# A float32 hybrid decoder layer on Trainium2: x and the norms' vectors loaded by channel instead of transposed on chip

## The chip, the cores and the metric

The kernel runs on one core of one Trainium2 chip. The metric is the device time of the kernel in microseconds (us), as the median of several executions. Engines are named as in the profile: PE is TensorE's matmuls and PEld its weight loads, DVE is VectorE, ACT is ScalarE, POOL is GpSimd, and SP is the engine whose queue issues nearly all DMAs.

## What is computed

One decoder layer on x of 256 tokens by 2048 channels, float32, batch 1:

```python
h = x
h = _layer_norm(ALPHA * h + 0.5 * _swiglu(h, ffn1_w_gate, ffn1_w_up, ffn1_w_down), ln_ffn1_g, ln_ffn1_b)
h = _layer_norm(ALPHA * h + _mixer(h, w_in, ...), ln_mix_g, ln_mix_b)
h = _layer_norm(ALPHA * h + 0.5 * _swiglu(h, ffn2_w_gate, ffn2_w_up, ffn2_w_down), ln_ffn2_g, ln_ffn2_b)

def _swiglu(x, w_gate, w_up, w_down):
    return (silu(x @ w_gate) * (x @ w_up)) @ w_down      # 2048 -> 5632 -> 2048
```

The mixer (sparse attention, dilated attention and gates) isn't touched by the change, except that two of its position tables (cmp_k_pos, cmp_v_pos) are among the vectors whose loading changes.

## The kernel before

**Arithmetic.** Every product of float32 matrices is made of three: operands are split into a rounded part (hi, float32r) and the rest (lo), and hi*hi, lo*hi and hi*lo are summed in PSUM. Weights stream from memory in slots of 512 KB: 2 blocks of 128 rows by 512 columns. For each slot SP loads `raw`, ACT rounds it into `w_hi` (round_slot, L491), DVE subtracts to get `w_lo` (split_slot, L505), and PE makes 12 matmuls of 512 columns (multiply_slot, L511: eight with w_hi on L519 and L520, four with w_lo on L525). `raw`, `w_hi` and `w_lo` are rings of 4 slots.

**What orders the ring.** Counting semaphores do. The load of slot n waits until `lo_done` has reached n - 3, that is until the low part of slot n - 4 is made (load_slot, L469). The rounding of slot n waits until `slots_used` has reached n - 3, that is until PE has finished slot n - 4 (L501). DVE waits for `hi_done`, PE for `hi_done` and then `lo_done`. Each engine works strictly in the order in which its program is written.

**The first feed-forward layer.** gu_chunk runs over 11 chunks of 512 hidden columns. A chunk has 16 slots: 8 of the gate weights into one accumulator pair, 8 of the up weights into the other. Chunk 0 is written apart (peel). After the gate half's last slot PE increments `slots_used` to 8; ACT then takes the tanh of the accumulator (L841, at s = 9, in ACT's order behind the rounding of slot 9 and ahead of that of slot 10), and DVE multiplies (L1070, behind the low part of slot 9 and ahead of that of slot 10). Later chunks run in a loop, then four down chunks of 22 slots each read hT_hi and hT_lo.

**x in the first chunk.** The products need x by channel (128 channels on partitions, 256 tokens in the free dimension), split into act_hi and act_lo. x lies in memory by token. SP loads it by token into `resid` in five parts (load_x, L705, 1 KB or 2 KB pieces), which is also the residual that the down projection is added to. PE transposes a pair of channel blocks at a time, four transpositions into one PSUM bank (x_task, L1584; transpose_pair, L554 to L560), ACT rounds the bank into act_hi (x_pairs, L860, through round_pair, L598), DVE subtracts into act_lo (L1092, through split_pair, L608). Pair 0 is transposed ahead of slot 0, pair 1 behind slot 0's high products, and pair s + 1 in the middle of slot s for s = 1 to 6. The identity for it, 64 KB, is the second load of SP (L717). In front of and behind the first transposition PE makes 6 and 5 warm-up products on zeros (keep_warm, L1610). The first two weight slots are loaded in halves (first_weights, L710).

**The vectors.** Four norm vectors and two position tables are loaded by row behind the load of slot 4 (load_vectors, L734), transposed by PE behind the first chunk (setup_task, L1704) and copied to `vecT` by DVE at s = 11 (L1059). Their readers are the later norms on ACT and the block sums on POOL.

**SP's order.** The loads of chunk 0 with those of x in between; load_ln(0), two DMAs of 1 MB; the loop of chunks; the down weights; then the mixer's.

Of the kernel before, what the change touches and what calls it, by code (L numbers as in the profile page):

```python
# [46 lines left out]
WARM_START = (6, 5)  # L47
X_FIRST = 2
IN_HALVES = 2
X_PARTS = ((0, 256), (256, 512), (512, 1024), (1024, 1536), (1536, D))  # L50
# [76 lines left out]
class Plan:  # L127


    def __init__(self):  # L130
        self.k, self.uses, self.t, self.at, self.by_pos = 0, [0] * BANKS, {}, {}, {}
        self.turn = list(range(BANKS))
# [9 lines left out]
def plan():  # L142
# [115 lines left out]
def build(nc, x, w1_gate, w1_up, w1_down, ln1_g, ln1_b, w_in, ck_pos, ck_w1, ck_w2, cv_pos, cv_w1, cv_w2,  # L258
          w_a, w_b, w_o, ln2_g, ln2_b, w2_gate, w2_up, w2_down, ln3_g, ln3_b, rope_c, masks_c, small_c, out):

    (w1_gate, w1_up, w1_down, ln1_g, ln1_b, w_in, ck_pos, ck_w1, ck_w2, cv_pos, cv_w1, cv_w2, w_a, w_b, w_o,
     ln2_g, ln2_b, w2_gate, w2_up, w2_down, ln3_g, ln3_b) = (
        a[0] for a in (w1_gate, w1_up, w1_down, ln1_g, ln1_b, w_in, ck_pos, ck_w1, ck_w2, cv_pos, cv_w1, cv_w2,
# [4 lines left out]
    with ctx:  # L268
# [9 lines left out]
        pos_rows = sb("pos_rows", [CMP_BLOCK, 2, P])  # L278
# [5 lines left out]
        at = 1152 + 4 * (160 + 128 + 256 + 128 + 48 + 16 + 8)  # L284
# [105 lines left out]
        x_loaded = [sem(f"x_loaded{q}") for q in range(len(X_PARTS))]  # L390
# [313 lines left out]
        def _(sp):  # L704
            def load_x(q):  # L705
                cs = slice(*X_PARTS[q])
                sp.dma_start(resid[:, :, cs], x[0].rearrange("(t p) d -> p t d", p=P)[:, :, cs]) \
                    .then_inc(x_loaded[q], 16)
# [25 lines left out]
            def load_vectors():  # L734
                for v, a in enumerate((ln1_g, ln1_b, ln2_g, ln2_b)):
                    sp.dma_start(vec_rows[16 * v:16 * v + 16, :], a.rearrange("(t p) -> t p", p=P)) \
                        .then_inc(consts_loaded, 16)
                sp.dma_start(pos_rows[:, 0, :], ck_pos).then_inc(consts_loaded, 16)
                sp.dma_start(pos_rows[:, 1, :], cv_pos).then_inc(consts_loaded, 16)
# [82 lines left out]
        def _(act):  # L822
            def gu_chunk(f, i, peel):
                per, c0 = 2 * GU_SLOTS, gu_acc[f]
                for s in range(2 * GU_SLOTS):
                    if peel and f == 0 and s <= X_FIRST:
                        x_pairs(s)
# [4 lines left out]
                    if peel and f == 0 and X_FIRST < s < GU_SLOTS:  # L832
                        x_pairs(s)
# [26 lines left out]
            def x_pairs(j):  # L860

                round_pair(act, ("x", 0, j), pair_of(act_hi, 2 * j))
# [171 lines left out]
        def _(dve):  # L1034
# [8 lines left out]
            def gu_chunk(f, i, peel):  # L1043
                per = 2 * GU_SLOTS
                for s in range(2 * GU_SLOTS):
                    if peel and f == 0 and s <= X_FIRST:
                        x_pairs(s)
# [4 lines left out]
                    if peel and f == 0 and X_FIRST < s < GU_SLOTS:  # L1052
                        x_pairs(s)
                    if peel and f == 1 and SPLIT <= s < GU_SLOTS:
                        split_piece(1, s + SPLIT)
                    if f == 0 and peel and s == 11:
                        t = T[("setup",)]
                        wait_filled(dve, t)
                        nc.vector.tensor_copy(vecT[:, :], bank[:, t.bank, 0:128]).then_inc(bank_emptied[t.bank], 1)  # L1059
# [151 lines left out]
            def down(f):  # L1211

                n_slots = OUT_CHUNKS * DOWN_SLOTS
                for s in range(n_slots):
# [368 lines left out]
        def _(pe):  # L1583
            def x_task(f, j):  # L1584
                t = T[("x", f, j)]
                if f == 0:
                    if j == 0:
                        pe.wait_ge(small_loaded, 16)
                    if j < 2 or j % 2 == 0:
                        pe.wait_ge(x_loaded[j if j < 2 else j // 2 + 1], 16)  # L1590
                wait_bank_free(pe, t)
                transpose_pair(resid, 2 * P * j, t.bank)

# [16 lines left out]
            def keep_warm(n):  # L1610

                for _ in range(n):
                    nc.tensor.matmul(bank[:, 3, 0:P], hid[:, 0, 0:P], hid[:, 0, 0:P], start=True, stop=True)

            def first_chunk(n0, c0):

                pe.wait_ge(zeros_ready, 1)
                keep_warm(WARM_START[0])
                x_task(0, 0)
                keep_warm(WARM_START[1])  # L1620
                for s in range(GU_SLOTS):
                    wait_moved(pe, T[("x", 0, s)])
                    first_chunk_slot(s, c0 % 2)

            def first_chunk_slot(s, pair):
# [3 lines left out]
                if s < IN_HALVES:  # L1629
                    pe.wait_ge(half_rounded, s + 1)  # L1630
                else:
                    pe.wait_ge(hi_done, s + 1)
                for k in range(SLOT_KT):
                    if k and 0 < s < GU_SLOTS - 1:
                        x_task(0, s + 1)
                    if k and s < IN_HALVES:
                        pe.wait_ge(hi_done, s + 1)
                    hi = b_hi[:, k * COLS:(k + 1) * COLS]
# [64 lines left out]

            def setup_task():  # L1704

                t = T[("setup",)]
                pe.wait_ge(consts_loaded, 16 * 6)
                wait_bank_free(pe, t)
                nc.tensor.transpose(bank[:, t.bank, 0:64], vec_rows[:, :], ident[0:64, 0:64])
                nc.tensor.transpose(bank[:, t.bank, 64:96], pos_rows[:, 0, :], ident[0:32, 0:32])  # L1710
                nc.tensor.transpose(bank[:, t.bank, 96:128], pos_rows[:, 1, :], ident[0:32, 0:32]).then_inc(bank_filled, 1)
# [300 lines left out]
        def _(pool):  # L2012
# [6 lines left out]

            for v in range(2):  # L2020
# [15 lines left out]
_INS = ["x", "ffn1_w_gate", "ffn1_w_up", "ffn1_w_down", "ln_ffn1_g", "ln_ffn1_b", "w_in", "cmp_k_pos", "cmp_k_w1",  # L2036
        "cmp_k_w2", "cmp_v_pos", "cmp_v_w1", "cmp_v_w2", "w_branch_a", "w_branch_b", "w_o", "ln_mix_g", "ln_mix_b",
        "ffn2_w_gate", "ffn2_w_up", "ffn2_w_down", "ln_ffn2_g", "ln_ffn2_b"]

# [16 lines left out]
```

## Time and profile before

| | |
|---|---|
| Median of 3 executions | 2217.81 us (2217.52 to 2217.85) |
| The profiled execution, its own time | 2217.98 us |
| Its span, first to last instruction | 2216.2 us |
| Mean granted clock of TensorE | 0.998 |
| Busy: PE, DVE, ACT | 2201.7 us, 1235.7 us, 959.6 us |
| Moved by DMA | 422.86 MB, mean 191 GB/s |

The rows below come from this one profiled execution. Starts are counted from the first instruction. A row of the timeline has the start, the duration, the engine, the line of the kernel, the operation, output and inputs, the shape and the count of what was merged; in brackets stands how long the engine had been idle and what released it. A matmul's duration contains its way through the array, so matmuls overlap: the distance between starts is what one costs. The granted clock (PEclk) is 1.00 for 2.4 GHz and 0.50 for 1.2 GHz.

### The profile page before, as it was taken

What the parts mean: (1) busy time and instruction counts of PE and PEld (TensorE: products, weight loads), DVE (VectorE), ACT (ScalarE), POOL (GpSimd) and SP (SyncE); (2) the same over time, 40 slices, a digit from 0 to 9 for tenths busy, and PEclk for the clock granted to TensorE, in tenths of its full rate; (3) what the DMA queues carried; (4) which work ended last, traced back from release to release, by engine and by line L of the source; (5) the groups of instructions that cost most, each with busy time, mean ns of one, the idle gap of its engine ahead of it and who ended that gap; (6) DMA issues with size and microseconds to landing.
All of it is one profiled execution on the core that took longest, in us unless ns stands there. A gap on an engine that the chain in (4) does not pass through costs nothing.

```text
span 2216.2 us, 27207 instructions
## 1 busy us (share of the span) xinstructions
PE 2201.7 (99%) x10137; PEld 1823.6 (82%) x10137; DVE 1235.7 (56%) x1230; ACT 959.6 (43%) x1126; POOL 7.7 (0%) x12
## 2 busy tenths in 40 slices
PE   9999999999999999999999999999999999999998
PEld 7888888888888888888888888888888888888886
DVE  5555455544544776776654556567555545545445
ACT  4344434443333644544345444364444444443333
POOL 0000000000000010000000000000000000000000
PEclk9999999999999999999999999999999999999999
DMA  7655665565666666665557566656655566566664
GB/s 270 206 184 188 190 191 185 188 191 190 195 192 193 186 188 206 188 184 161 169 163 208 171 204 206 196 166 195 197 188 180 188 197 188 180 236 193 196 191 142
DMA packets 224860, 422.86 MB, mean 191 GB/s; under 512 B 16400, under 2 KB 25872, under 8 KB 224016
## 3 DMA queue, kind: packets, MB, share of 16 engines
q1 hardware_dynamic: 224208, 420.76, 61.7%
q8 instruction: 52, 0.85, 0.2%
q10 hardware_dynamic: 576, 1.05, 0.1%
q14 instruction: 24, 0.20, 0.0%
HBM read 418.08 MB, written 3.68 MB: 190 GB/s over the span
## 4 chain that ended last, share of the span: by engine, by line
PE 98%; DVE 1%; ACT 0%; DMA 0%; issue 0%; SPq 0%; DVEq 0%; ACTq 0%
PE acc L519 31%; PE acc L520 31%; PE acc L525 31%; PE bank L558 1%; PE bank L1903 1%; PE bank L1743 0%; PE bank L1852 0%; PE bank L1874 0%; PE acc L1640 0%; PE acc L1641 0%; PE bank L1957 0%; PE acc L1647 0%; PE bank L1954 0%; DMA raw<-in_ffn_w_gate_dram 0%; PE bank L1856 0%; DVE w_lo L509 0%
## 5 line engine op out<-in xcount | busy, mean ns | idle before, releaser
L509 DVE TENSOR_TENSOR w_lo<-raw,w_hi 128x1024 fp32r<-128x1024 f32 x768 | 928.3, 1224 | 572.3 <-ACT w_hi L502 564.5
L502 ACT ACTIVATE w_hi<-raw 128x1024 fp32r<-128x1024 f32 x766 | 802.9, 1059 | 820.9 <-PE acc L525 775.0
L519 PE MATMUL acc<-w_hi,act_hi 128*128 128x512 f32 x2192 | 865.9, 395 | 0.0
L520 PE MATMUL acc<-w_hi,act_lo 128*128 128x512 f32 x2192 | 854.3, 390 | 0.0
L525 PE MATMUL acc<-w_lo,act_hi 128*128 128x512 f32 x2192 | 588.2, 389 | 0.1
L525 PEld LDWEIGHTS acc<-w_lo,act_hi 128*128 128x128 f32 x2192 | 411.3, 188 | 87.4 <-DVE w_lo L509 1.0
L519 PEld LDWEIGHTS acc<-w_hi,act_hi 128*128 128x128 f32 x2192 | 411.7, 188 | 86.7 <-issue 3.2
L520 PEld LDWEIGHTS acc<-w_hi,act_lo 128*128 128x128 f32 x2192 | 411.9, 188 | 82.1
L519 PE MATMUL acc<-w_hi,hT_hi 128*128 128x512 f32 x688 | 267.9, 389 | 0.0
L520 PE MATMUL acc<-w_hi,hT_lo 128*128 128x512 f32 x688 | 267.7, 389 | 0.0
L525 PE MATMUL acc<-w_lo,hT_hi 128*128 128x512 f32 x688 | 185.2, 389 | 0.0
L525 PEld LDWEIGHTS acc<-w_lo,hT_hi 128*128 128x128 f32 x688 | 129.2, 188 | 26.8
L520 PEld LDWEIGHTS acc<-w_hi,hT_lo 128*128 128x128 f32 x688 | 129.2, 188 | 26.7
L519 PEld LDWEIGHTS acc<-w_hi,hT_hi 128*128 128x128 f32 x688 | 129.1, 188 | 26.7
L1089 DVE TENSOR_TENSOR hT_lo<-bank,hT_hi 128x512 f32 (+1 forms) x44 | 30.3, 688 | 97.2 <-ACT hT_hi L858 97.2
L1070 DVE SCALAR_TENSOR_TENSOR gate_t<-gate_t,acc 128x1024 f32<-128x1024 f32 x22 | 26.9, 1222 | 88.7 <-ACT gate_t L841 88.7
L858 ACT ACTIVATE hT_hi<-bank 128x512 f32 (+1 forms) x44 | 26.2, 595 | 108.0 <-PE bank L558 108.0
L1081 DVE TENSOR_TENSOR hid<-gate_t,acc 128x1024 f32<-128x1024 f32 x22 | 26.9, 1222 | 65.0 <-PE acc L525 65.0
L841 ACT ACTIVATE gate_t<-acc 128x1024 f32<-128x1024 f32 x22 | 22.6, 1029 | 92.1 <-PE acc L525 90.1
L519 PE MATMUL acc<-w_hi,oT_hi 128*128 128x512 f32 x96 | 38.0, 395 | 0.0
L520 PE MATMUL acc<-w_hi,oT_lo 128*128 128x512 f32 x96 | 37.4, 390 | 0.0
L689 ACT ACTIVATE s<-s,negmax 128x128 f32<-128x128 f32 (+1 forms) x56 | 23.8, 430 | 26.8 <-DVE negmax L1310 26.8
(243 smaller groups left out, 842.2 us busy)
## 6 DMA issues: line engine op xcount, KB each, us to landing
raw<-in_ffn_w_up_dram SPq DMA_DIRECT2D x176, 512.0 KB, 4.5
raw<-in_ffn_w_down_dram SPq DMA_DIRECT2D x176, 512.0 KB, 4.5
raw<-in_w_in_dram SPq DMA_DIRECT2D x176, 512.0 KB, 4.2
raw<-in_ffn_w_gate_dram SPq DMA_DIRECT2D x174, 512.0 KB, 4.5
raw<-in_w_o_dram SPq DMA_DIRECT2D x32, 512.0 KB, 4.8
raw<-in_w_branch_a_dram SPq DMA_DIRECT2D x16, 512.0 KB, 5.1
raw<-in_cmp_k_w_dram SPq DMA_DIRECT2D x8, 512.0 KB, 4.0
raw<-in_cmp_v_w_dram SPq DMA_DIRECT2D x8, 512.0 KB, 4.0
```

The source lines that it names most:

```text
L502: nc.scalar.activation(weights(n0, s if isinstance(i, int) and i == 0 else s + per)[0], raw[:, r, :], ACT.Copy).then_inc(hi_done, 1)
L509: nc.vector.tensor_tensor(lo, raw[:, r, :], hi.bitcast(F32), ALU.subtract).then_inc(lo_done, 1)
L519: nc.tensor.matmul(o, a_hi[:, kt0 + k, at], hi, start=first and k == 0, stop=False)
L520: nc.tensor.matmul(o, a_lo[:, kt0 + k, at], hi, start=False, stop=False)
L525: mm = nc.tensor.matmul(o, a_hi[:, kt0 + k, at], lo, start=False, stop=last and k == SLOT_KT - 1)
L558: mm = nc.tensor.transpose(bank[:, b, k * TOKENS + tile * P:k * TOKENS + (tile + 1) * P], src[:, tile, col + k * P:col + (k + 1) * P], ident)
L689: nc.scalar.activation(v, v, ACT.Exp, bias=negmax[:, u, e:e + 1], scale=SCALE, accum_out=sums[:, u, e:e + 1]).then_inc(probs_ready, 1)
L841: nc.scalar.activation(gate_t[:, :, :], acc_pair(0), ACT.Tanh, scale=0.5).then_inc(gate_tanh, 1)
L858: nc.scalar.activation(dst, bank[:, half, :].rearrange("p (k n) -> p k n", k=2), ACT.Copy).then_inc(hi_moved, 1)
L1070: nc.vector.scalar_tensor_tensor(gate_t[:, :, :], gate_t[:, :, :], 1.0, acc_pair(0), ALU.add, ALU.mult).then_inc(acc_emptied[0], 1)
L1081: nc.vector.tensor_tensor(hid[:, :, :], gate_t[:, :, :], acc_pair(1), ALU.mult).then_inc(acc_emptied[1], 1)
L1089: nc.vector.tensor_tensor(hT_lo[:, k0, :], bank[:, half, :].rearrange("p (k n) -> p k n", k=2), hT_hi[:, k0, :].bitcast(F32), ALU.subtract ...
```

## The change

x is handed to the kernel in two layouts. Besides x by token there is a copy by channel (xT_c: row p holds, for each of the 16 channel blocks, the 256 tokens of channel p of the block), and one array vec_c that already holds what `vecT` has to hold. The kernel loads eight pairs of x by channel into x_raw, in memory that the hidden activations use later, each just ahead of the weights of its slot. ACT rounds and DVE subtracts from x_raw instead of from PSUM. The transpositions of x and of the vectors on PE are gone, and so is the copy of `vecT` on DVE. Eight warm-up products come in one group. x by token is loaded into `resid` in one DMA of 2 MB by SP behind the loop of chunks, ahead of the down weights, and DVE waits for it before the first add. The identity and `vecT` are loaded by load_constants, which SP reaches behind gu_chunk(0, 0) and ahead of load_ln(0); PE waits for the identity behind the first chunk, where the setup transposition was; ACT and POOL wait for `vecT` before they read it.

Since no bank is used for x any longer, the counts of tasks and of bank uses start at 1 instead, fed by the last warm-up product and by two memsets.

```diff
-WARM_START = (6, 5)
+WARM_START = 8
...
-        self.k, self.uses, self.t, self.at, self.by_pos = 0, [0] * BANKS, {}, {}, {}
+        self.k, self.uses, self.t, self.at, self.by_pos = 1, [1, 1, 0, 0], {}, {}, {}
...
-        for j in range(GU_SLOTS):
+        for j in range(GU_SLOTS if f else 0):
             task(("x", f, j), j % BANKS)
-        if f == 0:
-            task(("setup",), 2)
...
+        x_raw = chunks_lo[:, 0:4].rearrange("p a t (k n) -> p (a t k) n", n=TOKENS)
...
@@ sync
+            def load_x(j):
+                sp.dma_start(pair_of(x_raw, 2 * j), xT_c[:, 2 * j * TOKENS:(2 * j + 2) * TOKENS]).then_inc(x_loaded[j], 16)
...
-            load_x(0)
-            sp.dma_start(ident, small_c[:, n_small:]).then_inc(small_loaded, 16)
...
                         peel = f == 0 and isinstance(i, int) and h == 0
+                        if peel:
+                            load_x(s)
                         if peel and s < IN_HALVES:
                             first_weights(s)
                         else:
                             load_slot(sp, src, gu_slot[f], i, 2 * GU_SLOTS, h * GU_SLOTS + s)
-                        if peel:
-                            for q in ((1,), (2,), (), (3, 4))[s] if s < 4 else ():
-                                load_x(q)
-                            if s == 4:
-                                load_vectors()
...
+            def load_constants():
+                sp.dma_start(ident, small_c[:, n_small:]).then_inc(small_loaded, 16)
+                sp.dma_start(vecT[:, :], vec_c).then_inc(consts_loaded, 16)
 
             def ffn(f):
                 gu_chunk(f, 0)
                 if f == 0:
+                    load_constants()
                     load_ln(0)
                 with sp.Fori(1, GU_CHUNKS) as i:
                     gu_chunk(f, i)
-                if f == 1:
+                if f == 0:
+                    sp.dma_start(resid[:, :, :], x[0].rearrange("(t p) d -> p t d", p=P)).then_inc(resid_loaded, 16)
+                else:
                     sp.wait_ge(resid_ready, 2)
                     load_ln(2)
...
@@ scalar: x_pairs(s) stands ahead of the rounding of slot s for all s < 8
-                round_pair(act, ("x", 0, j), pair_of(act_hi, 2 * j))
+                act.wait_ge(x_loaded[j], 16)
+                nc.scalar.activation(pair_of(act_hi, 2 * j), pair_of(x_raw, 2 * j), ACT.Copy).then_inc(hi_moved, 1)
...
             def layer_norm_act(which):
+                act.wait_ge(consts_loaded, 16)
...
@@ vector: the same order
-                split_pair(dve, ("x", 0, j), pair_of(act_lo, 2 * j), pair_of(act_hi, 2 * j))
+                dve.wait_ge(hi_moved, moved[("x", 0, j)] + 1)
+                nc.vector.tensor_tensor(pair_of(act_lo, 2 * j), pair_of(x_raw, 2 * j), pair_of(act_hi, 2 * j).bitcast(F32),
+                                        ALU.subtract).then_inc(x_split, 1)
...
+                        if c == 0 and f == 0:
+                            dve.wait_ge(resid_loaded, 16)
...
+            for b in range(2):
+                nc.vector.memset(ln_s[:, 0, b:b + 1], 0.0).then_inc(bank_emptied[b], 1)
...
@@ tensor
-                keep_warm(WARM_START[0])
-                x_task(0, 0)
-                keep_warm(WARM_START[1])
+                keep_warm(WARM_START)
                 for s in range(GU_SLOTS):
-                    wait_moved(pe, T[("x", 0, s)])
                     first_chunk_slot(s, c0 % 2)
...
                 for k in range(SLOT_KT):
-                    if k and 0 < s < GU_SLOTS - 1:
-                        x_task(0, s + 1)
...
+                    pe.wait_ge(hi_moved, moved[("x", 0, s)] + 1)
                     for o, at in outs:
                         nc.tensor.matmul(o, act_hi[:, 2 * s + k, at], hi, start=s == 0 and k == 0, stop=False)
+                    pe.wait_ge(x_split, s + 1)
+                    for o, at in outs:
                         nc.tensor.matmul(o, act_lo[:, 2 * s + k, at], hi, start=False, stop=False)
-                if s == 0:
-                    x_task(0, 1)
...
                             first_chunk(n0, c0)
-                            setup_task()
+                            pe.wait_ge(small_loaded, 16)
...
@@ gpsimd
+            pool.wait_ge(consts_loaded, 16)
```

## Rows read from the trace of the kernel before

**Rows 1.** The page's first part: busy time of each engine.
```profile
PE 2201.7 (99%) x10137; PEld 1823.6 (82%) x10137; DVE 1235.7 (56%) x1230; ACT 959.6 (43%) x1126; POOL 7.7 (0%) x12
```
**Rows 2.** Waits of PE, whole execution: us in total, times, longest.
```profile
PE bank L1957 <- DVE w_lo L509: 1.1, 2, 0.8
...
PE acc L1640 <- ACT w_hi L848: 0.5, 1, 0.5
...
PE acc L1640 <- ACT w_hi L850: 0.4, 1, 0.4
```
**Rows 3.** Timeline of PE, start to 40 us: start, duration, what.
```profile
1.06 2.93 PE L1613 MATMUL bank<-hid 128*128 128x128 f32 x12 [1.06 <-DVE ln_s L1257]
...
4.46 1.28 PE L1613 MATMUL bank<-hid 128*128 128x128 f32 x10
...
10.87 0.50 PE L1640 MATMUL acc<-w_hi,act_hi 128*128 128x512 f32 x1 [0.49 <-DVE act_lo L608]
...
30.32 0.39 PE L1640 MATMUL acc<-w_hi,act_hi 128*128 128x512 f32 x1
...
32.13 1.07 PE L1647 MATMUL acc<-w_lo,act_hi 128*128 128x512 f32 x4
...
33.57 0.50 PE L519 MATMUL acc<-w_hi,act_hi 128*128 128x512 f32 x1
...
35.52 1.07 PE L525 MATMUL acc<-w_lo,act_hi 128*128 128x512 f32 x4
...
38.24 1.07 PE L525 MATMUL acc<-w_lo,act_hi 128*128 128x512 f32 x4
```
**Rows 4.** DMA issues at 1.26 and 2.23: count, size, us to landing.
```profile
small<-in_small_dram SPq DMA_DIRECT2D x1, 64.0 KB, 2.6
...
raw<-in_ffn_w_gate_dram SPq DMA_DIRECT2D x1, 256.0 KB, 4.9
```
**Rows 5.** Timeline of ACT in the first chunk and behind it.
```profile
7.14 0.63 ACT L850 ACTIVATE w_hi<-raw 128x512 fp32r<-128x512 f32 x1 [1.06 <-DMA raw<-in_ffn_w_gate_dram]
9.49 0.60 ACT L598 ACTIVATE act_hi<-bank 128x512 fp32r<-128x512 f32 x1 [1.71 <-PE bank L558]
...
33.24 1.03 ACT L841 ACTIVATE gate_t<-acc 128x1024 f32<-128x1024 f32 x1 [2.07 <-PE acc L1647]
34.16 2.00 ACT L502 ACTIVATE w_hi<-raw 128x1024 fp32r<-128x1024 f32 x2
```
**Rows 6.** Timeline of DVE in the first chunk and behind it.
```profile
7.88 1.23 DVE L509 TENSOR_TENSOR w_lo<-raw,w_hi 128x1024 fp32r<-128x1024 f32 x1 [1.91 <-ACT w_hi L850]
10.12 0.69 DVE L608 SCALAR_TENSOR_TENSOR act_lo<-bank,act_hi 128x512 fp32r<-128x512 f32 x1 [1.02 <-ACT act_hi L598]
...
34.30 1.22 DVE L1070 SCALAR_TENSOR_TENSOR gate_t<-gate_t,acc 128x1024 f32<-128x1024 f32 x1 [1.69 <-ACT gate_t L841]
35.44 2.35 DVE L509 TENSOR_TENSOR w_lo<-raw,w_hi 128x1024 fp32r<-128x1024 f32 x2
```
**Rows 7.** Windows: PE, PEld, DVE, ACT, POOL busy (count), PEclk, DMA share, GB/s.
```profile
13.00:14.00 1.00, 1.00 (x6) 0.75 (x4) 0.69 (x1) 1.00 (x3) 0.00 (x0) 1.00 1.07 416
```
**Rows 8.** Timeline of SP: loads of the up half, and the next DMA.
```profile
19.49 18.70 SPq L474 DMA_DIRECT2D raw<-in_ffn_w_up_dram  x8
38.23 0.47 SPq L759 DMA_DIRECT2D ln_nat<-in_ln_ffn_g_dram  x1
```
**Rows 9.** DMA landings: slot 15 (issued at 37.8), ln_nat behind it, median of all up loads.
```profile
raw<-in_ffn_w_up_dram SPq DMA_DIRECT2D x1, 512.0 KB, 6.8
ln_nat<-in_ln_ffn_g_dram SPq DMA_DIRECT2D x1, 1024.0 KB, 8.3
...
raw<-in_ffn_w_up_dram SPq DMA_DIRECT2D x176, 512.0 KB, 4.5
```
**Rows 10.** The last matmuls, and the window in which the granted clock falls.
```profile
2205.01 0.61 PE L525 MATMUL acc<-act_lo,hT_hi 128*128 128x512 f32 x2
...
2209.00:2209.50 0.50, 0.00 (x0) 0.00 (x0) 0.50 (x1) 0.44 (x2) 0.00 (x0) 0.55 0.00 0
```

More of the change, by code:

```diff
@@ L45 @@
 LAST_SPLIT = 8
-WARM_START = (6, 5)
-X_FIRST = 2
+WARM_START = 8
 IN_HALVES = 2
-X_PARTS = ((0, 256), (256, 512), (512, 1024), (1024, 1536), (1536, D))
 SPLIT = 4
@@ L255, in mixer_constants, with build @@
             np.ascontiguousarray(small, np.float32))
-def build(nc, x, w1_gate, w1_up, w1_down, ln1_g, ln1_b, w_in, ck_pos, ck_w1, ck_w2, cv_pos, cv_w1, cv_w2,
+def build(nc, x, xT_c, vec_c, w1_gate, w1_up, w1_down, ln1_g, ln1_b, w_in, ck_w1, ck_w2, cv_w1, cv_w2,
           w_a, w_b, w_o, ln2_g, ln2_b, w2_gate, w2_up, w2_down, ln3_g, ln3_b, rope_c, masks_c, small_c, out):
-    (w1_gate, w1_up, w1_down, ln1_g, ln1_b, w_in, ck_pos, ck_w1, ck_w2, cv_pos, cv_w1, cv_w2, w_a, w_b, w_o,
+    (w1_gate, w1_up, w1_down, ln1_g, ln1_b, w_in, ck_w1, ck_w2, cv_w1, cv_w2, w_a, w_b, w_o,
      ln2_g, ln2_b, w2_gate, w2_up, w2_down, ln3_g, ln3_b) = (
-        a[0] for a in (w1_gate, w1_up, w1_down, ln1_g, ln1_b, w_in, ck_pos, ck_w1, ck_w2, cv_pos, cv_w1, cv_w2,
+        a[0] for a in (w1_gate, w1_up, w1_down, ln1_g, ln1_b, w_in, ck_w1, ck_w2, cv_w1, cv_w2,
                        w_a, w_b, w_o, ln2_g, ln2_b, w2_gate, w2_up, w2_down, ln3_g, ln3_b))
@@ L277, in build @@
         vec_rows = sb("vec_rows", [64, P])
-        pos_rows = sb("pos_rows", [CMP_BLOCK, 2, P])
         vecT = sb("vecT", [P, 4 * KT + 2 * CMP_BLOCK])
@@ L282, in build @@
         mv = sb("mv", [P, TILES, 2])
-        at = 1152 + 4 * (160 + 128 + 256 + 128 + 48 + 16 + 8)
+        at = 1152 + 4 * (160 + 128 + 128 + 48 + 16 + 8)
         if at % 512:
@@ L389, in build @@
         hi_moved = sem("hi_moved")
-        x_loaded = [sem(f"x_loaded{q}") for q in range(len(X_PARTS))]
+        x_loaded = [sem(f"x_loaded{j}") for j in range(GU_SLOTS)]
+        x_split = sem("x_split")
+        resid_loaded = sem("resid_loaded")
         small_loaded = sem("small_loaded")
@@ L704, in _ @@
         def _(sp):
[L705 to L708, printed above, removed]
+            def load_x(j):
+                sp.dma_start(pair_of(x_raw, 2 * j), xT_c[:, 2 * j * TOKENS:(2 * j + 2) * TOKENS]).then_inc(x_loaded[j], 16)
             def first_weights(s):
@@ L727, in gu_chunk @@
                             load_slot(sp, src, gu_slot[f], i, 2 * GU_SLOTS, h * GU_SLOTS + s)
-                        if peel:
-                            for q in ((1,), (2,), (), (3, 4))[s] if s < 4 else ():
-                                load_x(q)
-                            if s == 4:
-                                load_vectors()
[L734 to L739, printed above, removed]
+            def load_constants():
+                sp.dma_start(ident, small_c[:, n_small:]).then_inc(small_loaded, 16)
+                sp.dma_start(vecT[:, :], vec_c).then_inc(consts_loaded, 16)
             def ffn(f):
@@ L825, in gu_chunk @@
                 for s in range(2 * GU_SLOTS):
-                    if peel and f == 0 and s <= X_FIRST:
+                    if peel and f == 0 and s < GU_SLOTS:
                         x_pairs(s)
@@ L831, in gu_chunk @@
                         round_slot(act, gu_slot[f], i, per, s)
-                    if peel and f == 0 and X_FIRST < s < GU_SLOTS:
-                        x_pairs(s)
                     if peel and f == 1 and SPLIT <= s < GU_SLOTS:
@@ L1045, in gu_chunk @@
                 for s in range(2 * GU_SLOTS):
-                    if peel and f == 0 and s <= X_FIRST:
+                    if peel and f == 0 and s < GU_SLOTS:
                         x_pairs(s)
@@ L1051, in gu_chunk @@
                         split_slot(dve, gu_slot[f], i, per, s)
-                    if peel and f == 0 and X_FIRST < s < GU_SLOTS:
-                        x_pairs(s)
                     if peel and f == 1 and SPLIT <= s < GU_SLOTS:
                         split_piece(1, s + SPLIT)
[L1056 to L1059, printed above, removed]
                     if peel and f == 1 and s >= 10:
@@ L1583, in _ @@
         def _(pe):
[L1584 to L1592, printed above, removed]
             def norm_task(f, j):
@@ L1612, in keep_warm @@
                 for _ in range(n):
-                    nc.tensor.matmul(bank[:, 3, 0:P], hid[:, 0, 0:P], hid[:, 0, 0:P], start=True, stop=True)
+                    mm = nc.tensor.matmul(bank[:, 3, 0:P], hid[:, 0, 0:P], hid[:, 0, 0:P], start=True, stop=True)
+                mm.then_inc(bank_filled, 1)
             def first_chunk(n0, c0):
                 pe.wait_ge(zeros_ready, 1)
-                keep_warm(WARM_START[0])
-                x_task(0, 0)
-                keep_warm(WARM_START[1])
+                keep_warm(WARM_START)
                 for s in range(GU_SLOTS):
-                    wait_moved(pe, T[("x", 0, s)])
                     first_chunk_slot(s, c0 % 2)
@@ L1628, in first_chunk_slot @@
                 outs = [(acc[:, 2 * pair + tile, :], slice(tile * P, (tile + 1) * P)) for tile in range(TILES)]
[L1629 to L1632, printed above, removed]
                 for k in range(SLOT_KT):
-                    if k and 0 < s < GU_SLOTS - 1:
-                        x_task(0, s + 1)
-                    if k and s < IN_HALVES:
+                    hi = b_hi[:, k * COLS:(k + 1) * COLS]
+                    if s < IN_HALVES and k == 0:
+                        pe.wait_ge(half_rounded, s + 1)
+                    else:
                         pe.wait_ge(hi_done, s + 1)
-                    hi = b_hi[:, k * COLS:(k + 1) * COLS]
+                    pe.wait_ge(hi_moved, moved[("x", 0, s)] + 1)
                     for o, at in outs:
                         nc.tensor.matmul(o, act_hi[:, 2 * s + k, at], hi, start=s == 0 and k == 0, stop=False)
+                    pe.wait_ge(x_split, s + 1)
+                    for o, at in outs:
                         nc.tensor.matmul(o, act_lo[:, 2 * s + k, at], hi, start=False, stop=False)
-                if s == 0:
-                    x_task(0, 1)
                 pe.wait_ge(lo_done, s + 1)
@@ L1702, in gu_chunk @@
                                 h_task(f, i, half)
[L1704 to L1711, printed above, removed]
             def ffn(f):
@@ L2033, in _, with by_partition @@
                 ins.then_inc(blk_ready, 1)
-_INS = ["x", "ffn1_w_gate", "ffn1_w_up", "ffn1_w_down", "ln_ffn1_g", "ln_ffn1_b", "w_in", "cmp_k_pos", "cmp_k_w1",
-        "cmp_k_w2", "cmp_v_pos", "cmp_v_w1", "cmp_v_w2", "w_branch_a", "w_branch_b", "w_o", "ln_mix_g", "ln_mix_b",
+_INS = ["ffn1_w_gate", "ffn1_w_up", "ffn1_w_down", "ln_ffn1_g", "ln_ffn1_b", "w_in", "cmp_k_w1", "cmp_k_w2",
+        "cmp_v_w1", "cmp_v_w2", "w_branch_a", "w_branch_b", "w_o", "ln_mix_g", "ln_mix_b",
         "ffn2_w_gate", "ffn2_w_up", "ffn2_w_down", "ln_ffn2_g", "ln_ffn2_b"]
+def by_partition(a):
+    n = a.shape[0]
+    return np.ascontiguousarray(a.reshape(n, -1, P).transpose(2, 1, 0)).reshape(P, -1)
 def kernel(**inputs):
@@ L2045 @@
     nc = bacc.Bacc("TRN2", target_bir_lowering=False, num_devices=1, dynamic_dma_scratch_size=1024)
-    named = [(name, np.ascontiguousarray(inputs[name])) for name in _INS]
+    x = np.ascontiguousarray(inputs["x"])
+    vectors = [by_partition(np.asarray(inputs[name])) for name in ("ln_ffn1_g", "ln_ffn1_b", "ln_mix_g", "ln_mix_b")]
+    vectors += [np.asarray(inputs[name])[0].T for name in ("cmp_k_pos", "cmp_v_pos")]
+    named = [("x", x), ("x_by_channel", by_partition(x[0])), ("vectors", np.ascontiguousarray(np.concatenate(vectors, 1)))]
+    named += [(name, np.ascontiguousarray(inputs[name])) for name in _INS]
     named += list(zip(("rope", "masks", "small"), mixer_constants()))
```

## The prediction, on record before the changed kernel was run

> **What bounds the kernel now.** I read the page's busy times first: TensorE is busy for 99% of the span, VectorE for little more than half [rows 1]. The waits of TensorE come next: the largest group behind the very first instruction is 1.1 us in two pieces, and the others are waits of about half a microsecond for the first slots' operands [rows 2]. So TensorE's own work is the time, and a change pays only by taking work off TensorE or by removing the few gaps at the front, and it costs whatever new wait it gives TensorE. The third view is the order of TensorE's instructions at the start [rows 3]. Two groups of low-part products lie 2.72 us apart where nothing but weights is multiplied (35.52 and 38.24): that is a slot of twelve matmuls, 0.227 us each, and every slot of the first chunk above this is what the change can win. The slots of the first chunk take longer: from 10.87 to 30.32 there are six of them, 3.24 us each.
>
> **Step 1, slot 0.** Before, slot 1 begins at 10.87 [rows 3]. Ahead of it stand the second half of slot 0's weights (issued at 2.23, 4.9 us to landing, so 7.13 [rows 4]), its rounding from 7.14 for 0.63 [rows 5], its low part on VectorE from 7.88 for 1.23 [rows 6], then transposition, rounding and splitting of x's second pair in series. Afterwards the identity's load no longer stands ahead of the weights: two SP issues of about 0.5 us become one, and 64 KB go. The second half is issued at about 1.72. With the same 4.9 us it lands at 6.6; x now comes in 2 KB pieces per partition instead of 1 KB ones and there is less in front, so I take 6.3. Rounding to 6.98, low part from 7.1 to 8.3, its four matmuls to 9.3. The second pair of x is there as raw channels, so its rounding (0.60 us [rows 5]) and its split (0.69 [rows 6]) run under slot 0, and slot 1 begins at 9.3. Bounds: 9.0 and 10.4 (the old time less the 0.5 us of the issue, if x or slot 1's halves are what comes last). The eight warm-up calls are 16 passes from 1.06 on; they end before the first product, as the old ones did, and cost nothing; the weights cover them.
>
> **Step 2, slots 1 to 7.** The six transpositions between the products go: 19.45 us for six slots becomes 6 x 2.72 = 16.32, a gain of 3.1. From slot 7's start to its last group it is 1.81 (30.32 to 32.13), unchanged. So the last group of the first chunk, call its start M, moves from 32.13 to 9.3 + 16.32 + 1.81 = 27.43: 4.7 us earlier. What could eat this are the transfers: 768 KB are wanted per 2.72 us, 290 GB/s, against 416 GB/s where the queues are full [rows 7]. ACT spends 0.60 + 1.0 us and DVE 0.69 + 1.2 on a slot with its x pair [rows 5, 6]. Both fit; I charge 0.
>
> **Step 3, the setup transposition.** Before, the up half begins at 33.57, M + 1.44; the four matmuls of M's group need 0.91. So removing the three small transpositions gives 0.53.
>
> **Step 4, the new wait, the largest term.** Behind the first chunk TensorE waits for small_loaded, and the identity is now loaded by load_constants, which SP reaches only after it has issued all 16 slots of chunk 0. SP does not run that far ahead. The load of slot 15 waits for the low part of slot 11; slot 11 is rounded only when slot 7 is used up, and ACT does the gate's tanh first. The trace shows this chain: tanh at 33.24, two roundings from 34.16 [rows 5]; the gate's product on DVE at 34.30, two low parts from 35.44 for 2.35 [rows 6], thus to 37.79; then the eighth up load, and at 38.23 the next DMA in SP's order, ln_nat [rows 8]. That is the place the identity takes: M + 6.10. None of this chain waits for the up half of TensorE, so it is no deadlock, and nothing in it gets shorter. With M at 27.43 the issue is at 33.53. Queued behind the waiting TensorE are all products of the up half; ACT and DVE follow to slot 11 and then stand too, having no used slot to refill. Hence nothing is recouped.
> The landing of the identity at that place is not in the trace. At the kernel's start the same 64 KB took 2.6 us [rows 4]. Slot 15's 512 KB, issued 0.4 us before our place, took 6.8 us, with ln_nat's 2 MB behind it [rows 9]; the identity has those 2 MB behind it too. These are the bounds; I take 4.2, a little nearer the low one, since a small transfer need not wait for all of the large one's stragglers. TensorE resumes at 33.53 + 4.2 = 37.73 where it was at 33.57: +4.2 with steps 1 to 3 included (-5.2 for them, +9.4 for the wait).
> The Trainium skill (DMA: Bandwidth & Descriptors, Queues, rings and completion order) says that a DMA's semaphore lands only after every earlier write of the same engine. By that the identity cannot be seen before slot 15 is in, and the sum would be that of the third rival; no row here shows a small load right behind such a large one.
>
> **Step 5, the clock.** TensorE stands for some 9 us. At the end of the kernel its last matmuls start at 2205.01, and the granted clock falls from 1.00 to 0.50, the 1.2 GHz level, within 2209.0 to 2209.5 [rows 10], less than 4 us after them. So it restarts at half speed. How long this lasts shows at the kernel's start: 12 passes took 2.93 us, 0.24 each, the later 10 took 1.28, 0.13 each [rows 3]; the column says 1.00 there, but the durations say half. Half of 2.93 is lost: +1.5. Bounds 0 (it may come back at once) and 3.0 (twice as long).
>
> **At nothing.** x by token, 2 MB on SP before the down weights: ln_nat's 2 MB behind chunk 0 delay the following slots in just this way and no wait of TensorE shows there [rows 2]; the first reader is some 60 us later. If the ring's lead were gone it would cost up to 5 us (2 MB at 416 GB/s). vecT by DMA takes one copy off DVE; its new waits on ACT and POOL come tens of us after it. Two more memsets on DVE at the start are under 0.1 us each, under the loads. The plan's banks and turns stay as they were, so the mixer is untouched.
>
> **Sum.** The profiled execution took 2217.98 (span 2216.2); 2217.98 + 4.2 + 1.5 = 2223.7. The median of the runs is 0.17 lower; I give 2223.6.
>
> **Rivals.** First, on the other side: SP has the identity issued in time, so TensorE goes from chunk to chunk without a stop. Place: SP's order behind slot 15. Price: no wait, no clock loss, -5.2, 2212.8. For it: steps 1 to 3 are read from rows, and SP does run about four slots ahead elsewhere. Against: slot 15's load hangs on slot 11's low part, and the issue at M + 6.1 is a row. It decides when wait and clock together are under 5.2 us, which needs an issue about 3 us or more before that place even with the shortest landing.
> Second, a short wait: landing in 2.6 us and a clock that is back within 1 us: 2217.98 + 2.6 + 0.5 = 2221.1, no difference to be measured. For it: the identity is small, and the start shows 2.6. Against: up to two 512 KB loads stand in front.
> Third, a long wait: the identity lands with slot 15, which before was at 37.8 + 6.8 = 44.6, or M + 12.5. TensorE resumes at 39.9: +6.3, with the clock 1.5: 2225.8. For it: the 6.8 itself. Against: the median landing of all 176 up loads is 4.5 us [rows 9], and the 2 MB of ln_nat now come about 1 us later.
>
> **How the numbers follow.** A measurement can tell about 0.2%, 4.4 us. The forecast, landing within about 3 to 5 us, has 0.50; the long wait 0.28; the short one 0.18; no wait 0.04. So slower 0.78, within 0.2% 0.18, faster 0.04. With all low bounds the sum is +2.3 (front -0.3, landing -1.6, clock -1.5), with all high ones +10.9; both ends need everything at once. The range holds the middle of each: 2220.8 to 2227.4, leaving out the first rival and the extreme corners.
>
> **What would show it.** TensorE's waits list a new one of 8 to 11 us at the first matmul of the up half, released by the DMA into small; SP issues that DMA about 6.1 us behind the start of the last first-chunk group; a stretch of granted clock 0.50 begins in the gap, and the first products behind it have twice the distance. First-chunk slots are 2.72 us apart from about 9.3, with M near 27.4. The landing of the identity is the term to read first. The forecast is wrong if the identity is issued well before the first chunk ends, if a second wait shows in the first chunk (x or weights late), or if the down projection waits for its weights behind x by token.

## The result, and the profile after

| | before | after |
|---|---|---|
| Median | 2217.86 us (2217.52 to 2218.12, 8 runs) | 2225.23 us (2224.57 to 2226.54, 8 runs) |
| Profiled execution | 2217.98 us | 2226.54 us |
| Span, mean granted clock | 2216.2 us, 0.998 | 2224.7 us, 0.996 |

The ratio is 1.0033, with a 95% interval of 1.0024 to 1.0042: the change makes the kernel slower by 7.4 us. Forecast were 2223.6 us and slower; the time lies inside the range, 1.6 us above the forecast. The profiled execution of after is the slowest of its eight, so its terms below add up to 8.6 us, not 7.4.

The lines of the changed file have moved: what was L501 to L525 is one line less, L1640 and L1641 are L1617 and L1620, L1647 is L1624, L1613 is L1595, the tanh L841 is L831, the gate product L1070 is L1056.

TensorE's waits over the whole execution, as [rows 2] for before (us in total, times, longest):

```profile
PE acc L518 <- DMA small<-in_small_dram: 10.1, 1, 10.1
...
PE acc L1617 <- ACT w_hi L501: 0.8, 1, 0.8
PE acc L1617 <- ACT w_hi L838: 0.6, 1, 0.6
PE acc L524 <- DVE w_lo L508: 0.3, 1, 0.3
```

The first line is new and is by itself larger than the whole loss. Its place is in the timeline of TensorE, which answers to [rows 3]:

```profile
1.06 3.53 PE L1595 MATMUL bank<-hid 128*128 128x128 f32 x16 [1.06 <-DVE ln_s L1249]
5.21 0.73 PE L1617 MATMUL acc<-w_hi,act_hi 128*128 128x512 f32 x2 [0.62 <-ACT w_hi L838]
...
8.42 0.72 PE L1617 MATMUL acc<-w_hi,act_hi 128*128 128x512 f32 x2
...
12.35 0.73 PE L1617 MATMUL acc<-w_hi,act_hi 128*128 128x512 f32 x2 [0.81 <-ACT w_hi L501]
...
26.09 0.62 PE L1617 MATMUL acc<-w_hi,act_hi 128*128 128x512 f32 x2
...
27.90 1.07 PE L1624 MATMUL acc<-w_lo,act_hi 128*128 128x512 f32 x4
39.05 0.79 PE L518 MATMUL acc<-w_hi,act_hi 128*128 128x512 f32 x1 [10.08 <-DMA small<-in_small_dram]
39.64 0.63 PE L519 MATMUL acc<-w_hi,act_lo 128*128 128x512 f32 x1
40.07 0.63 PE L518 MATMUL acc<-w_hi,act_hi 128*128 128x512 f32 x1
...
46.56 1.07 PE L524 MATMUL acc<-w_lo,act_hi 128*128 128x512 f32 x4
47.47 0.39 PE L518 MATMUL acc<-w_hi,act_hi 128*128 128x512 f32 x1
```

The last group of the first chunk starts at 27.90 instead of 32.13: the front works. Then TensorE stands until 39.05, and its first products behind that are 0.43 us apart instead of 0.23.

The chain that holds the identity, in the timelines of ACT, DVE and SP, as [rows 5, 6, 8]:

```profile
29.01 1.02 ACT L831 ACTIVATE gate_t<-acc 128x1024 f32<-128x1024 f32 x1 [4.25 <-PE acc L1624]
29.93 1.99 ACT L501 ACTIVATE w_hi<-raw 128x1024 fp32r<-128x1024 f32 x2
44.63 1.06 ACT L501 ACTIVATE w_hi<-raw 128x1024 fp32r<-128x1024 f32 x1 [12.71 <-PE acc L524]
```

```profile
30.07 1.22 DVE L1056 SCALAR_TENSOR_TENSOR gate_t<-gate_t,acc 128x1024 f32<-128x1024 f32 x1 [4.05 <-ACT gate_t L831]
31.20 2.36 DVE L508 TENSOR_TENSOR w_lo<-raw,w_hi 128x1024 fp32r<-128x1024 f32 x2
45.72 1.23 DVE L508 TENSOR_TENSOR w_lo<-raw,w_hi 128x1024 fp32r<-128x1024 f32 x1 [12.17 <-ACT w_hi L501]
```

```profile
17.46 16.49 SPq L473 DMA_DIRECT2D raw<-in_ffn_w_up_dram  x8
33.99 0.47 SPq L727 DMA_DIRECT2D small<-in_small_dram  x1
```

Tanh, two roundings, gate product, two low parts, slot 15's load, identity: the same order as before, and the issue is 6.09 us behind the start of the last group, where ln_nat stood 6.10 behind it [rows 8]. ACT and DVE then stand for 12 us as well (12.71 and 12.17 in brackets), so no work is done ahead by which the stop could be made good later.

DMA landings of slot 15's load (issued at 33.59) and of the identity behind it, and windows of the granted clock (PEclk is the third number from the end):

```profile
raw<-in_ffn_w_up_dram SPq DMA_DIRECT2D x1, 512.0 KB, 5.2
small<-in_small_dram SPq DMA_DIRECT2D x1, 64.0 KB, 5.0
```

```profile
31.50:32.00 0.50, 0.00 (x0) 0.00 (x0) 0.50 (x1) 0.42 (x1) 0.00 (x0) 0.50 0.00 0
...
43.00:44.00 1.00, 1.00 (x4) 0.75 (x3) 0.00 (x0) 0.00 (x0) 0.00 (x0) 0.50 0.14 57
45.00:45.50 0.50, 0.50 (x3) 0.37 (x3) 0.00 (x0) 0.50 (x1) 0.00 (x0) 0.85 0.00 0
```

The clock is at 0.50 (1.2 GHz) from 31.5 on and comes back shortly after 45.0, six microseconds behind the restart.

### The profile page after: what moved, and what is told of

It is laid out like the page before. It is cut to its first block, busy times and chain, and to the rows that moved or that the text cites. A ratio compares the mean times of both kernels' runs of the same rounds, so it can differ in the third digit from the quotient of the medians.

```text
span 2224.7 us, 27140 instructions
## 1 busy us (share of the span) xinstructions
PE 2199.9 (99%) x10096; PEld 1821.2 (82%) x10096; DVE 1235.6 (56%) x1231; ACT 959.4 (43%) x1126; POOL 7.7 (0%) x12
## 4 chain that ended last, share of the span: by engine, by line
PE 97%; DVE 1%; DMA 1%; ACT 0%; SPq 0%; issue 0%; DVEq 0%; ACTq 0%
PE acc L518 31%; PE acc L519 30%; PE acc L524 30%; PE bank L557 1%; PE bank L1871 1%; PE bank L1711 0%; PE bank L1820 0%; PE bank L1842 0%; DVE w_lo L508 0%; DMA raw<-in_ffn_w_gate_dram 0%; PE bank L1925 0%; PE bank L1922 0%; PE acc L1617 0%; PE acc L1624 0%; PE acc L1620 0%; DMA small<-in_small_dram 0%
## 5 line engine op out<-in xcount | busy, mean ns | idle before, releaser
L501 ACT ACTIVATE w_hi<-raw 128x1024 fp32r<-128x1024 f32 x766 | 802.4, 1058 | 835.2 <-PE acc L524 776.9
L518 PE MATMUL acc<-w_hi,act_hi 128*128 128x512 f32 x2192 | 867.1, 396 | 10.1 <-DMA small<-in_small_dram 10.1
L1056 DVE SCALAR_TENSOR_TENSOR gate_t<-gate_t,acc 128x1024 f32<-128x1024 f32 x22 | 26.9, 1221 | 91.1 <-ACT gate_t L831 91.1
L831 ACT ACTIVATE gate_t<-acc 128x1024 f32<-128x1024 f32 x22 | 22.6, 1028 | 94.3 <-PE acc L524 90.1
```

Source lines behind the costliest of these rows:

```text
L501: nc.scalar.activation(weights(n0, s if isinstance(i, int) and i == 0 else s + per)[0], raw[:, r, :], ACT.Copy).then_inc(hi_done, 1)
L518: nc.tensor.matmul(o, a_hi[:, kt0 + k, at], hi, start=first and k == 0, stop=False)
L831: nc.scalar.activation(gate_t[:, :, :], acc_pair(0), ACT.Tanh, scale=0.5).then_inc(gate_tanh, 1)
L1056: nc.vector.scalar_tensor_tensor(gate_t[:, :, :], gate_t[:, :, :], 1.0, acc_pair(0), ALU.add, ALU.mult).then_inc(acc_emptied[0], 1)
```

## The experiments

The theory was that the late identity and the clock it costs are the whole loss, and that the front gains some 5 us. Rivals: that x by token or the new traffic costs something too; that the slow products behind the stop have another cause; that a DMA of 64 KB has its own latency of 5 us; that the transpositions were not what the front gained. The ratios stand against the kernel before on the same chip, 2217.95 us for the first four runs and 2217.85 us for the last four.

**The wait moved to its first use.**

```diff
-                            pe.wait_ge(small_loaded, 16)
...
                         if not peel and h == 0 and s == 3:
+                            if f == 0:
+                                pe.wait_ge(small_loaded, 16)
                             for half in range(2):
                                 h_task(f, i, half)
```

> The changed kernel with TensorE's wait for the identity moved from behind the first chunk to its first use, the transposition of the hidden activations in the loop. Loads stay where they are. My theory (the late identity and the clock drop are the whole loss): no stop behind the first chunk, granted clock 1.00 throughout the front, about 4.9 us faster than the kernel before (first chunk's last group at 27.9 where it was at 32.13, 4.2, and 0.5 for the setup transposition), 2213.0 us. Rival (x by token ahead of the down weights, or the bigger traffic, costs something of its own, hidden now by the stop's refilled ring): a new wait appears later and the gain is under 4 us, 2214 us or more.

Measured: 2213.32 us (2212.63 to 2213.89), ratio 0.9979 (0.9970 to 0.9988). Its timeline of TensorE across the end of the first chunk:

```profile
27.95 1.07 PE L1624 MATMUL acc<-w_lo,act_hi 128*128 128x512 f32 x4
28.86 0.39 PE L518 MATMUL acc<-w_hi,act_hi 128*128 128x512 f32 x1
```

One wait moved by some 30 us of TensorE's own work turns 7.4 us lost into 4.6 us won. The up half starts 4.71 us earlier than before (28.86 for 33.57), and the profiled execution, 2213.32 us, is 4.66 us below the profiled one of before. So nothing of the front's gain is given back later: x by token, 2 MB more, is hidden, as charged.

**The constants issued early.** SP runs load_constants() behind the load of slot 7, the wait stays behind the first chunk.

```diff
+                        if peel and s == GU_SLOTS - 1:
+                            load_constants()
...
                 if f == 0:
-                    load_constants()
                     load_ln(0)
```

> The changed kernel with the identity and vecT issued by SP behind the load of slot 7 instead of behind slot 15; TensorE's wait stays behind the first chunk. My theory: the identity is issued near 16 us and has landed long before 28.8 us even in full queues, so the same time as with the wait moved, 2213.0 us within 0.5. Rival (a wait there costs by itself, or the two loads delay the weights of the first chunk): 1 us or more above that run.

Measured: 2213.57 us (2212.58 to 2214.12), ratio 0.9979 (0.9970 to 0.9988), the same as with the wait moved. A wait for something that has landed costs nothing that shows here; place of issue and place of wait are two cures for one fault.

**TensorE kept busy in the gap.**

```diff
                             first_chunk(n0, c0)
+                            for _ in range(38):
+                                nc.tensor.matmul(bank[:, 3, 0:P], hid[:, 0, 0:P], hid[:, 0, 0:P], start=True, stop=True)
                             pe.wait_ge(small_loaded, 16)
```

> The changed kernel with 38 more warm-up products of zeros behind the first chunk, ahead of the wait for the identity. They take about 9.5 us of the 10.1 us in which TensorE stands, so the stop is as long but the clock should stay up. My theory: the granted clock stays 1.00, TensorE resumes at about 39.0 us as before but at full distance, and the time falls by what the clock cost: 3.0 us against the profiled execution of the changed kernel, 2 to 3 us against its median: 2222.2 to 2223.2 us. Rival (the slow first products behind the stop are due to something else, such as the DMA traffic then): no change, 2225 us.

Measured: 2223.46 us (2223.09 to 2225.81), ratio 1.0026 (1.0016 to 1.0035). TensorE:

```profile
28.90 8.64 PE L1670 MATMUL bank<-hid 128*128 128x128 f32 x76
38.49 0.50 PE L518 MATMUL acc<-w_hi,act_hi 128*128 128x512 f32 x1 [0.94 <-DMA small<-in_small_dram]
38.83 0.40 PE L519 MATMUL acc<-w_hi,act_lo 128*128 128x512 f32 x1
39.07 0.40 PE L518 MATMUL acc<-w_hi,act_hi 128*128 128x512 f32 x1
```

The window behind the stop, PEclk third from the end:

```profile
39.00:40.00 1.00, 1.00 (x6) 0.77 (x6) 0.00 (x0) 0.00 (x0) 0.00 (x0) 1.00 1.03 434
```

76 products whose result is not used make the kernel 1.8 us faster than the change by the medians, a little under the 2 to 3 us expected, and the products behind the stop are back at 0.23 us. The granted clock stayed at 1.00 while the DMAs moved as much as behind the stop of the changed kernel (434 and 395 GB/s from 39 to 40). So the clock was the cause of the slow products, and not the traffic. From resuming to the low-part group of the second up slot it takes 4.70 us here (38.49 to 43.19) and 7.51 in the changed kernel (39.05 to 46.56): 2.8 us in that execution. The medians say 1.8; the cost differs from run to run. The next kernel gives the cleanest pair: its TensorE resumes at the same 38.49 with the clock at 0.50, takes 6.83 us over the same two slots, 2.13 more, and its profiled execution is longer by 2.13 us as well (2225.22 and 2223.09).

**The identity without the 2 MB behind it.**

```diff
                 sp.dma_start(ident, small_c[:, n_small:]).then_inc(small_loaded, 16)
+                sp.wait_ge(small_loaded, 16)
                 sp.dma_start(vecT[:, :], vec_c).then_inc(consts_loaded, 16)
```

> The changed kernel with SP waiting for the identity before it issues vecT and ln_nat, so that no 2 MB are queued behind it. SP's place of issue stays, near 34.0 us. If the traffic behind the identity delayed it (slot 15 took 5.2 us, the identity 5.0): it lands in about 3.5 us and TensorE resumes 1.5 us earlier, about 2223.7 us. If what counts is what stands ahead of it (slots 14 and 15) or a fixed latency: 5.0 us to landing as before, 2225.2 us.

Measured: 2225.16 us (2224.4 to 2226.3), ratio 1.0032 (1.0020 to 1.0043), no change. The identity took 4.6 us instead of 5.0. What stands behind it hardly matters (3.5 us was expected if it did), so what is left is what stands ahead of it, or a latency of its own.

**The identity ahead of slot 15.**

```diff
+                        if f == 0 and isinstance(i, int) and h == 1 and s == GU_SLOTS - 2:
+                            sp.dma_start(ident, small_c[:, n_small:]).then_inc(small_loaded, 16)
...
             def load_constants():
-                sp.dma_start(ident, small_c[:, n_small:]).then_inc(small_loaded, 16)
```

> The changed kernel with the identity issued by SP between the loads of slots 14 and 15, one DVE low part (1.2 us) earlier than in the change. In the changed kernel it landed 0.2 us behind slot 15's 512 KB, which was issued just ahead of it. If a small load is seen only once the large load ahead of it is in: it now lands just behind slot 14, whose load took 3.6 us from 32.4, at about 36.2 us; TensorE resumes some 2.8 us earlier and the time is 2222.4 us. If the landing is a latency of its own of about 5 us: issue near 32.8, landing near 37.8, 1.2 us earlier, 2224.0 us.

Measured: 2222.74 us (2221.90 to 2223.52), ratio 1.0021 (1.0012 to 1.0030), 2.5 us below the change where 2.8 were expected. Landings of slot 14's load (issued at 33.17) and of the identity (33.58):

```profile
raw<-in_ffn_w_up_dram SPq DMA_DIRECT2D x1, 512.0 KB, 3.7
small<-in_small_dram SPq DMA_DIRECT2D x1, 64.0 KB, 3.5
```

The identity's time to landing fell from 5.0 to 3.5 us, with the load ahead of it: 33.58 + 3.5 = 37.1, slot 14 at 36.9. In the profiles of all four kernels with the stop it landed 0.1 to 0.3 us behind the large load in front. It has no latency of its own of 5 us; it was seen when the load ahead of it was in. The Trainium skill (DMA: Bandwidth & Descriptors, Queues, rings and completion order) says that the increment of a DMA's semaphore lands only after every earlier write of the same DMA engine, and that DMAs of one issuing engine need not complete in their order for all that. The four traces agree with the first; no run here shows the second.

**Slot 2's weights in halves too**, on the kernel with the wait at its use.

```diff
-IN_HALVES = 2
+IN_HALVES = 3
```

> The kernel with the wait at its use, and slot 2's weights loaded and rounded in halves like those of slots 0 and 1 (IN_HALVES 3). TensorE stood 0.9 us ahead of slot 2 for its rounding. If the half's earlier landing and its shorter rounding (0.63 instead of 1.06 us) are what was late: the wait falls to 0.3 us or less and the time by 0.5 us or more, 2212.8 us. If the transfer of the whole slot is the limit: the wait moves to the second half, no change, 2213.3 us.

Measured: 2212.42 us (2212.0 to 2213.74), ratio 0.9975 (0.9966 to 0.9985), 5.4 us below the kernel before and the fastest version found. It is 0.9 us below the kernel with the wait at its use, by medians of 10 and 11 runs whose ranges overlap (2212.0 to 2213.74 and 2212.63 to 2213.89). No wait ahead of slot 2 is left in its profile, but that execution, the slowest of the ten, ran the whole of slot 0 at half speed, which hides such a wait. So the 0.9 us rest on the medians, and that they are this wait is likely and not shown.

**The transpositions put back**, on the kernel with the wait at its use. The transposed data are zeros and aren't used.

```diff
+                    if k == 0 and 0 < s < GU_SLOTS - 1:
+                        pe.wait_ge(small_loaded, 16)
+                        for q in range(4):
+                            nc.tensor.transpose(bank[:, 3, q * P:(q + 1) * P], hid[:, 0, 0:P], ident)
...
+            act.dma_start(ident, small_c[:, TILES * N_CMP + TILES:]).then_inc(small_loaded, 16)
```

> The kernel with the wait at its use, with four transpositions of zeros into a free bank put back into the middle of each of slots 1 to 6, as the kernel before had them; the identity is loaded by ACT's queue at the start, and the results are not used. In the kernel before, such slots took 3.20 instead of 2.72 us. If this was the transpositions' own price: 6 x 0.48 = 2.9 us, less up to 0.5 us that slot 1's hide in the wait ahead of slot 2: 2215.9 to 2216.3 us. If the chain from transposition over ACT and DVE back to TensorE was part of it: less than 2.0 us, under 2215.3 us.

Measured: 2216.63 us (2215.05 to 2217.09), ratio 0.9993 (0.9984 to 1.0002). Slots 3 and 4 in its timeline:

```profile
16.69 0.62 PE L1617 MATMUL acc<-w_hi,act_hi 128*128 128x512 f32 x2
17.14 0.62 PE L1620 MATMUL acc<-w_hi,act_lo 128*128 128x512 f32 x2
17.60 0.60 PE L1624 MATMUL bank<-small,hid 128*128 128x128 f32 x4
17.96 0.71 PE L1617 MATMUL acc<-w_hi,act_hi 128*128 128x512 f32 x2
...
19.89 0.62 PE L1617 MATMUL acc<-w_hi,act_hi 128*128 128x512 f32 x2
```

That is 3.20 us per slot with no consumer of the result. Before the change slots 3 to 6 took the same, from here to slot 7's start at 30.32:

```profile
17.51 0.39 PE L1640 MATMUL acc<-w_hi,act_hi 128*128 128x512 f32 x1
```

So the price in these slots was TensorE's own time, 0.48 us for four transpositions and the change of operand, and not the chain over ACT and DVE. The median is 3.3 us above the kernel without them, 0.3 to 0.7 more than expected. In the profile the first product comes at 5.73 instead of 5.20 and slot 0 runs at half speed; the extra load of the identity at the start may be behind the first, and it wasn't tried alone.

**x's pairs 1 and 2 on ACT's queue**, on the same kernel.

```diff
                         if peel and s not in (1, 2):
                             load_x(s)
...
+            for j in (1, 2):
+                act.dma_start(pair_of(x_raw, 2 * j), xT_c[:, 2 * j * TOKENS:(2 * j + 2) * TOKENS]).then_inc(x_loaded[j], 16)
             act.wait_ge(zeros_ready, 3)
```

> The kernel with the wait at its use, with x's pairs 1 and 2 issued by ACT's queue at the start instead of by SP, so that SP issues slot 2's weights about 1 us earlier. If the issue rate limits the first slots: the 0.9 us ahead of slot 2 disappear, 2212.5 us. If the rate of the transfers does (about 300 GB/s from 4 to 9 us): the wait stays above 0.6 us, and slot 0 may even start later because x competes with its weights, 2213.3 us or more.

Measured: 2214.73 us (2214.29 to 2215.64), ratio 0.9985 (0.9976 to 0.9994), 1.4 us slower than the kernel with the wait at its use. TensorE's first product, and a window behind it:

```profile
6.68 0.73 PE L1619 MATMUL acc<-w_hi,act_hi 128*128 128x512 f32 x2 [2.07 <-ACT w_hi L838]
```

```profile
8.00:9.00 1.00, 1.00 (x3) 0.81 (x4) 1.00 (x1) 1.00 (x3) 0.00 (x0) 0.50 1.04 404
```

It starts at 6.68 instead of 5.20, because ACT began to round x's pair 0 at 4.93 instead of 3.88 and slot 0's weights at 6.00 instead of 4.52, both released by their loads. The loads that TensorE needs first land 1.1 to 1.5 us later when more is issued beside them. What was to disappear did: slot 2's weights are rounded at 9.76 instead of 11.30, and no wait of TensorE stands ahead of that slot. But the granted clock fell to 0.50 between 7.5 and 8 and came back at about 11, so that slot 0 took 4.58 us and not 3.40, and the up half starts at 30.34 instead of 28.86. The issue order, the queue and the clock all changed, so this run doesn't tell whether the issue or the transfers made slot 2 late. It does show that some 300 GB/s was no ceiling: from 2 to 9 us it moved 336 GB/s, where the kernel with the wait at its use moved 291.

## Why the prediction was right, and where it was off

The sum against the profiled execution, in us (the forecast's last step is rounded up: 2223.68 less 0.17 is 2223.5, and 2223.6 was given):

| Term | Forecast | Measured |
|---|---|---|
| First chunk (27.90 for 32.13) and setup transposition (0.53), steps 1 to 3 | -5.2 | -4.8 |
| Stop: issue behind the last group's start | 6.10 | 6.09 |
| Stop: from issue to TensorE's resumption | 4.2 | 5.06 |
| Stop in all (step 4) | +9.4 | +10.2 |
| Clock (step 5) | +1.5 | +2.8 |
| Sum | +5.7 | +8.2, of 8.6 in all |

The other 0.3 us were not found. The front, the landing and the clock all came out worse than forecast. That the median is only 1.6 us off is in part because the profiled execution is the slowest of its eight: by the medians the clock cost 1.8.

**Mechanism and sign.** The prediction named the stop, the order of SP that causes it, and its length to within 0.9 us. The place of issue was right to 0.01 us, and not by luck: it is 6.09 us in the kernels with TensorE busy in the gap and with the identity alone too. It came from finding what stood at that place in the trace of before, and from checking that nothing in the chain to it depends on the work that the wait holds up.

One of the prediction's own signs of being wrong did show: a second wait in the first chunk, 0.8 us ahead of slot 2, for weights that were late. It belongs to step 2 and is small beside the stop.

**Step 1** was too late by 0.9: slot 1 began at 8.42, not 9.3, because the second half of the weights was being rounded at 5.33 (6.3 was the landing taken, [rows 4] had 7.1).

**Step 2** was too hopeful where it charged 0 for transfers. From slot 1 to slot 2 it was 3.93 us, not 2.72: slot 2's weights took 7.2 us from their issue at 4.05, and ACT could round them only at 11.24. The 416 GB/s of [rows 7] is the rate at 13 us; from 4 to 8 us both kernels move 239 to 332 GB/s. The two errors go against each other and leave the last group at 27.90 for 27.43. Loading and rounding slot 2 in halves then won 0.9 by the medians.

**Step 4's landing** was mis-sized: 5.0 for 4.2. I had put it nearer the low bound because a small transfer need not wait for all of a large one's stragglers. Here it did: the identity landed with the load ahead of it in every such profile. The third rival had the mechanism right. Its number, 6.4 us, was too long only because slot 15 itself took 5.2 us this time and not 6.8; why, no run shows (4.6 and 4.9 in two of the other kernels with the stop).

The prediction says that no row shows a small load right behind a large one. The trace of before had such rows. At its start, the load of x ahead of the identity was issued at 0.75:

```profile
resid<-in_x_dram SPq DMA_DIRECT2D x1, 256.0 KB, 2.9
small<-in_small_dram SPq DMA_DIRECT2D x1, 64.0 KB, 2.6
```

It lands at 3.65 and the identity, issued at 1.26, at 3.86, 0.2 us behind it: the low bound of 2.6 us was itself the time of the load ahead. And behind slot 4's load, issued at 9.13, stood six loads of 8 and 16 KB; the first and the last of them:

```profile
raw<-in_ffn_w_gate_dram SPq DMA_DIRECT2D x1, 512.0 KB, 8.0
vec_rows<-in_ln_ffn_g_dram SPq DMA_DIRECT2D x1, 8.0 KB, 6.9
...
pos_rows<-in_cmp_v_pos_dram SPq DMA_DIRECT2D x1, 16.0 KB, 6.5
```

All six took 6.2 to 6.9 us. On these rows the third rival was the better choice for this step.

**Step 5** was mis-sized too. The slow stretch behind the restart was 6.1 us in the profile and not 2.9; its cost was 2.8, 2.1 and 1.7 us in the profiles of the change, of the identity alone and of the identity ahead of slot 15, measured from resuming to the same group (7.51, 6.83 and 6.44 us against 4.70), and 1.8 by the medians. The one stretch at the kernel's start from which I took 2.9 was a short one of a wide spread (last section).

**At nothing** was right: with the stop gone, the gain at 29 us arrives whole at the end.

**The rivals.** The first, no stop, is what the wait at its use gives: 2213.3 us, where 2212.8 was worked out; it just isn't what the change does. The second, a landing of 2.6 us, fell: the shortest landing of the identity behind a load of 512 KB was 3.5 us.

## What to carry to other kernels

When a load is moved behind others, ask first what its issuing queue is held by at that place; the trace of before shows it as the issue time of whatever stands there now. Then ask how much work that doesn't need the load stands behind the wait for it, and put the wait behind that work: here the cure was one line of SP's order or one line of TensorE's, worth 12 us (2225.2 to 2213.3). The 64 KB load landed with the large one ahead of it in every profile here in which SP issued the two one behind the other, so take the large one's landing for it. And the stops of 7.4 to 10.1 us cost a further 1.7 to 2.8 us of slow products behind them.

## What was not expected of the hardware

In the first microseconds the granted clock's column can read 1.00 while TensorE runs at half speed. In the kernel with the identity ahead of slot 15 the first slot ran at half speed (pairs of products 0.85 us apart, as behind the stop at a granted clock of 0.50, until about 10), with the column at 1.00 in the same window; the first line is TensorE's timeline, the second the window:

```profile
8.11 1.05 PE L1621 MATMUL acc<-w_hi,act_lo 128*128 128x512 f32 x2
```

```profile
8.00:9.00 1.00, 1.00 (x4) 0.71 (x4) 0.28 (x1) 0.61 (x1) 0.00 (x0) 1.00 0.95 311
```

The same start of the program reached full speed at about 4 us in one kernel's profile (the change), at 6 in another's (the wait at its use) and at 10 in a third's (this one). In the kernel with x on two queues the column does show the half speed that sets in behind 7.5 us. Some of the spread of 1 to 2 us between runs of one kernel may be this; it wasn't tested.
